# Two seven-product weight slabs: which engine forms the weight sums, where the raw blocks lie, and when the head squares run

## The chip, the cores and the metric

The kernel runs on one core of one Trainium2 chip. The metric is the device time of one execution in microseconds (us). A difference is read against the three runs of the kernel before, 1936.15 to 1937.51 us.

## The reference, cut to what matters

Two transformer blocks over 512 tokens of width 1024 in float32. The change touches the even layer of the second one:

```python
h = rmsnorm_2(x, pre_g)
u = h @ w_in.astype(jnp.float32)
qa, ka, va, oa, za, ia, fa, qb, kb, vb, zb = split_cols(u, EVEN_SPLITS)
...
ha = mlstm(qa.reshape(hs), ka.reshape(hs), va.reshape(hs), ig, lf)
ha = jax.nn.sigmoid(oa) * ha
ya = head_norm(ha, hn_g, A_HEADS) * jax.nn.silu(za)
```

`oa` and `za` are 512 x 1024 each: 512 tokens, contraction over 1024, 1024 columns. `head_norm` divides each of the 4 heads (256 wide) of a token by the root of the mean of its squares.

## The kernel before, in words

Every weight matrix is read in raw blocks of 128 rows by 512 columns of float32 (256 KB). A block becomes two operands: a high part, made by ScalarE's cast (L766, `w_hi_of`), and a low part, raw minus high, made by GpSimd for ordinary slabs (L713) and by VectorE for the seven-product slabs (L2063). TensorE takes three matmuls for each product of blocks: high by high, high by low, low by high. High and low parts have eight places each, taken in turn by block number; a cast waits until the block eight before has been used by TensorE (`wait_used`). Raw blocks of ordinary slabs lie in a ring of eight slots, `w_raw`; a slot is loaded again by SyncE (L605) when the low part of the block that had it is made.

`oa` and `za` are computed by two slabs of class `Seven`, `lstm_o` and then `lstm_z`. Tokens, contraction and columns are each halved, which gives 2 x 2 quarters of the weight matrix, q11, q12, q21, q22, of four raw blocks each, and four quarters of the result. Seven products of quarters replace the usual eight, in the Strassen-Winograd manner. The weight operands, in the order of the products, are B11 = q11, T1 = q11 + q12, T2 = T1 + q22, B21 = q21, T3 = q12 + q22, B22 = q22, T4 = T2 + q21; the signs are in the token operands, which VectorE and ScalarE make ahead of the slabs. One product is 4 blocks x 2 token tiles x 3 matmuls = 24 matmuls of 512 columns. An ordinary slab of eight blocks has 12 matmuls for each.

The raw blocks before: B11, T1, T2 and T4 share one buffer of four blocks, `kept`, used by both slabs. q11 is loaded into it (L615), for the second slab only after T4 of the first has given up its blocks. GpSimd then adds q12 and later q22 with accumulating DMAs (`weight_sums`, L744), each block when VectorE has made the low part of the sum that it held. T3 and B22 lie in the ring; VectorE adds T3 = q12 + q22 there (`add_t3`, L2048) between the low parts of B21. q21 lies in `b21` (L622), and VectorE adds it for T4 (`add_t4`, L2053) between the low parts of T3.

Products are summed in PSUM: banks `work` 0 and 1 and `proj` 0 to 3. Between products ScalarE seeds T2's banks with a copy of B11's product (`b_from_a`, L1280) and saves T1's product (`own_from_c`, L1288); VectorE seeds B22's banks from T2's product (`c_from_b`, L2074), for which T3 waits, and forms the second quarter of the result from T3's product (`own_from_b`, L2081), for which T4 waits. As each quarter of the result is complete ScalarE applies the gate (`gate`, L1307) and VectorE multiplies (`gated_quarter`, L2096 and L2101).

Each engine's order is written out by hand: on ScalarE by the calls of `prepared_to`, `gate` and the copies, on VectorE by `rests`, `c_from_b`, `own_from_b` and `gated_quarter`. SyncE issues plain loads in one queue in order of blocks, GpSimd its DMAs in another. Ahead of the two slabs TensorE works off the slab `sb_q` (eight blocks); behind them come `sb_k`, whose first block is followed by the transposes of the gated heads (L2498), and `sb_v`. The head squares of `head_norm` (L1342) are ScalarE's, 16 of 128 x 256, eight before and eight after the T3 casts of the second slab, all in the table set that also holds the square root.

## Time and profile before

| | us |
|---|---|
| median of 3 runs | 1937.35 |
| lowest, highest | 1936.15, 1937.51 |
| profiled execution, its own time | 1936.78 |
| its span | 1935.0 |
| TensorE busy | 1915.9 |
| VectorE busy | 790.0 |
| ScalarE busy | 811.0 |
| GpSimd busy | 951.1 |

The span runs from the first to the last instruction of the execution; its own time is 1.78 us longer. Times of the trace are counted from the span's start. The two seven-product slabs lie between 1239.00 and 1323.96 us.

### The profile page before, as it was taken

The numbers are of one execution on the slowest core, as the hardware profiler recorded it, in microseconds if no ns is written. First come the engines' busy times: TensorE is split into PE (matmuls) and PEld (weight loads), VectorE is DVE, ScalarE is ACT, GpSimd is POOL, SyncE is SP. The second block draws the span as 40 slices with busy tenths as digits, with TensorE's granted clock in tenths as the row PEclk, the third lists the DMA queues.
The fourth block names the chain that finished last, engine by engine and source line by source line (L and its number), as shares of the span: only waits on it lengthen the run. The fifth ranks groups of instructions, "written<-read, shape, count | busy, mean of one in ns | idle before, by whom it ended". The sixth has DMA issues, their size and how long they took to land.

```text
span 1935.0 us, 25859 instructions
## 1 busy us (share of the span) xinstructions
PE 1915.9 (99%) x9142; PEld 1607.0 (83%) x9142; DVE 790.0 (41%) x1264; ACT 811.0 (42%) x1585; POOL 951.1 (49%) x1237
## 2 busy tenths in 40 slices
PE   9999999999999999999999999999999999999998
PEld 7878888998888988888889888877888888888887
DVE  2430321340123223323247854766356646014652
ACT  5522443423324333333356543355456646333332
POOL 5733544534365555665545733115344455555572
PEclk9999999999999999999999999999999999999999
DMA  6342433323133323333342320554222242333331
GB/s 233 104 107 54 123 88 87 88 66 85 57 109 109 121 88 92 100 106 103 98 131 70 106 76 23 131 136 125 61 77 71 71 136 74 101 92 93 96 111 54
DMA packets 102849, 186.44 MB, mean 96 GB/s; under 512 B 11068, under 2 KB 16808, under 8 KB 102750
## 3 DMA queue, kind: packets, MB, share of 16 engines
q1 hardware_dynamic: 94676, 170.41, 30.1%
q10 hardware_dynamic: 5770, 10.49, 1.7%
q0 software_dynamic: 2304, 4.20, 1.3%
q8 instruction: 64, 1.05, 0.2%
q14 instruction: 35, 0.29, 0.0%
HBM read 179.03 MB, written 6.02 MB: 96 GB/s over the span
## 4 chain that ended last, share of the span: by engine, by line
PE 90%; DVE 5%; ACT 2%; DMA 2%; issue 1%; POOL 0%; SPq 0%; DVEq 0%; ACTq 0%; POOLq 0%
PE proj L2325 26%; PE proj L2327 26%; PE proj L2326 26%; DMA arena<-in_w_in_ab 2%; PE work L2325 1%; PE work L2326 1%; PE work L2327 1%; PE work L2896 1%; PE work L2877 1%; DVE w_lo L2063 1%; PE work L2701 1%; ACT w_hi L766 1%; PE work L2498 1%; PE work L2852 1%; PE work L2420 1%
## 5 line engine op out<-in xcount | busy, mean ns | idle before, releaser
L713 POOL TENSOR_TENSOR w_lo<-w_raw,w_hi 128x256 fp32r<-128x256 f32 x1200 | 931.9, 809 | 877.6 <-ACT w_hi L766 761.8
L2325 PE MATMUL proj<-act_hi,w_hi 128*128 128x512 f32 (+1 forms) x1312 | 495.8, 378 | 0.6 <-DVE arena L1775 0.3
L2327 PE MATMUL proj<-act_hi,w_lo 128*128 128x512 f32 (+1 forms) x1312 | 490.4, 374 | 0.0
L2326 PE MATMUL proj<-act_lo,w_hi 128*128 128x512 f32 (+1 forms) x1312 | 490.3, 374 | 0.0
L766 ACT CAST w_hi<-w_raw 128x512 fp32r<-128x512 f32 x520 | 304.1, 619 | 398.9 <-PE proj L2327 369.7
L2325 PEld LDWEIGHTS proj<-act_hi,w_hi 128*128 128x128 f32 x1312 | 247.1, 188 | 44.6 <-DVE arena L1775 0.7
L2327 PEld LDWEIGHTS proj<-act_hi,w_lo 128*128 128x128 f32 x1312 | 247.0, 188 | 44.3
L2326 PEld LDWEIGHTS proj<-act_lo,w_hi 128*128 128x128 f32 x1312 | 247.2, 188 | 43.7 <-issue 0.5
L2325 PE MATMUL proj<-w_hi,act_hi 128*128 128x512 f32 x640 | 257.5, 402 | 1.2 <-DVE arena L2187 1.0
L2327 PE MATMUL proj<-w_hi,act_lo 128*128 128x512 f32 x640 | 250.2, 391 | 0.0
L2326 PE MATMUL proj<-w_lo,act_hi 128*128 128x512 f32 x640 | 249.9, 391 | 0.0
L2325 PEld LDWEIGHTS proj<-w_hi,act_hi 128*128 128x128 f32 x640 | 128.0, 200 | 25.3 <-issue 2.1
L2325 PE MATMUL proj<-w_hi,aux_hi 128*128 128x512 f32 x368 | 146.1, 397 | 2.9 <-ACT arena L904 1.9
L2327 PEld LDWEIGHTS proj<-w_hi,act_lo 128*128 128x128 f32 x640 | 128.0, 200 | 23.1
L2326 PEld LDWEIGHTS proj<-w_lo,act_hi 128*128 128x128 f32 x640 | 128.2, 200 | 22.8 <-issue 1.0
L2327 PE MATMUL proj<-w_hi,aux_lo 128*128 128x512 f32 x368 | 143.4, 390 | 0.0
L2326 PE MATMUL proj<-w_lo,aux_hi 128*128 128x512 f32 x368 | 143.3, 389 | 0.0
L1118 ACT CAST w_hi<-w_raw 128x512 fp32r<-128x512 f32 x96 | 57.4, 622 | 126.2 <-PE proj L2327 125.9
L1823 DVE TENSOR_TENSOR arena<-arena 128x512 f32<-128x512 f32 x32 | 26.3, 821 | 144.3 <-ACT arena L1088 144.3
L2307 DVE TENSOR_TENSOR arena<-arena 128x512 f32<-128x512 f32 x40 | 35.6, 890 | 120.2 <-ACT arena L1466 119.3
L2325 PEld LDWEIGHTS proj<-w_hi,aux_hi 128*128 128x128 f32 x368 | 69.1, 188 | 18.5 <-POOL w_lo L713 3.5
L2326 PEld LDWEIGHTS proj<-w_lo,aux_hi 128*128 128x128 f32 x368 | 69.1, 188 | 14.8 <-issue 0.7
(396 smaller groups left out, 2241.9 us busy)
## 6 DMA issues: line engine op xcount, KB each, us to landing
w_raw<-in_w_in SPq DMA_DIRECT2D x154, 256.0 KB, 2.7
w_raw<-in_w_in_ab SPq DMA_DIRECT2D x130, 256.0 KB, 2.7
w_raw<-in_w_mlp SPq DMA_DIRECT2D x128, 256.0 KB, 2.8
w_raw<-in_w_in_c SPq DMA_DIRECT2D x64, 256.0 KB, 2.7
w_raw<-in_w_out_ab SPq DMA_DIRECT2D x32, 256.0 KB, 2.8
w_raw<-in_w_out_c SPq DMA_DIRECT2D x32, 256.0 KB, 2.8
w_raw<-in_w_o_gla SPq DMA_DIRECT2D x16, 256.0 KB, 2.7
w_raw<-in_w_out SPq DMA_DIRECT2D x16, 256.0 KB, 2.7
```

The source lines that it names most:

```text
L713: ins = pool.tensor_tensor(w_lo[:, slot, c], raw_of(b)[:, c], w_hi[:, slot, c].bitcast(F32), ALU.subtract)
L766: act.copy(w_hi[:, b % RING, :], raw_of(b)).then_inc(hi_ready, 1)
L1118: act.copy(w_hi[:, b % RING, :], raw_of(b)).then_inc(hi_ready, 1)
L1823: vec.tensor_tensor(relu_sq[:, c % 2, :], relu[:, c, :], relu[:, c, :], ALU.mult).then_inc(squared, 1)
L2063: vec.tensor_tensor(w_lo[:, b % RING, :], raw_of(b), w_hi[:, b % RING, :].bitcast(F32), ALU.subtract)\
L2307: step(vec.tensor_tensor(dst[:, POOL_PAD:], src[:, POOL_PAD:], src[:, POOL_PAD - back:PADDED - back], ALU.add))
L2325: pe.matmul(out_, a_hi, b_hi, start=first, stop=False)
L2326: pe.matmul(out_, a_hi, b_lo, start=False, stop=False)
L2327: return pe.matmul(out_, a_lo, b_hi, start=False, stop=last)
L2420: ins = pe.transpose(work[:, 2 * (m % 2) + b, (k % 4) * P:(k % 4 + 1) * P], normed_x[name][:, m, k * P:(k + 1) * P], ident[:])
L2498: ins = pe.transpose(work[:, k % 4, m * P:(m + 1) * P], src[:, m, c:c + P], ident[:])
L2701: ins = pe.matmul(work[:, 3, t], att_v[g][:, kb, h * HD:(h + 1) * HD], att_pt[g][:, at * P:(at + 1) * P], start=(g == 0 and n == 0), stop= ...
```

## The change

The sums T2 and T4, which stand in a chain, are now VectorE's: `add_t2` between the low parts of T1, `add_t4` between those of B21. The accumulating DMAs make T1 and T3, each one behind the plain load of its first summand. B11, B21 and T3 lie in the ring, T3 being summed in its slot. `kept` holds T1, T2 and T4 and has a place of its own for each slab; `held` holds q22 for T2 and B22. Each slab has 20 plain loads where it had 16, and 8 accumulating DMAs as before. A ring slot that held B21 is loaded again when `add_t4` has read it. The head squares are made in four groups of four, after the gates of the first slab; scratch for them lies in free parts of the arena.

```diff
-        super().__init__(name, q11 + q12 + q22 + q21 + q12 + q22 + q21, 4)
+        super().__init__(name, q11 + q11 + 4 * [None] + q21 + q12 + q22 + 4 * [None], 4)
+        self.added = {T1: q12, T3: q22}
...
-            s.kept, s.b21, s.own = view(0, 4, NCOL), view(10240, 4, NCOL), view(2048, 2, NCOL)
+        for s, kept_at in zip(sevens, (0, 14336)):
+            s.kept, s.held, s.own = view(kept_at, 4, NCOL), view(10240, 4, NCOL), view(2048, 2, NCOL)
+        head_squares_at = (12288, 13312, 0, 1024)
...
                 if ring_no[b] >= RING:
-                    wait_lo(sp, ring_order[ring_no[b] - RING])
+                    before_ = ring_order[ring_no[b] - RING]
+                    s, j = blocks[before_]
+                    if isinstance(s, Seven) and j // 4 == B21:
+                        sp.wait_ge(block_added, 8 * sevens.index(s) + 4 + j % 4 + 1)
+                    else:
+                        wait_lo(sp, before_)
...
             def load_seven(s):
                 at = sevens.index(s)
-                if s is sevens[0]:
+                def ring_loads(p):
+                    for k in range(4):
+                        load(s.first_of(p) + k, s.sources[4 * p + k])
+                ring_loads(B11)
+                if at == 0:
                     sp.wait_ge(proj_full, end("lstm_core"))
                 for k in range(4):
-                    if s is not sevens[0]:
-                        wait_lo(sp, sevens[at - 1].first_of(T4) + k)
-                    sp.dma_start(s.kept[:, k, :], s.sources[k]).then_inc(kept_loaded[k], 16)
-                for p in (T3, B22):
-                    for k in range(4):
-                        load(s.first_of(p) + k, s.sources[4 * p + k])
+                    sp.dma_start(s.kept[:, k, :], s.sources[4 * T1 + k]).then_inc(kept_loaded[k], 16)
+                if at:
+                    ring_loads(B21)
                 for k in range(4):
-                    if s is not sevens[0]:
-                        sp.wait_ge(block_added, 8 * at - 4 + k + 1)
-                    sp.dma_start(s.b21[:, k, :], s.sources[4 * B21 + k]).then_inc(b21_loaded[k], 16)
+                    if at:
+                        wait_lo(sp, sevens[at - 1].first_of(B22) + k)
+                    sp.dma_start(s.held[:, k, :], s.sources[4 * B22 + k]).then_inc(held_loaded[k], 16)
+                if at == 0:
+                    ring_loads(B21)
+                ring_loads(T3)
...
             def weight_sums(s):
-                for p in (T1, T2):
-                    for k in range(4):
-                        wait_lo(pool, s.first_of(p - 1) + k)
-                        pool.dma_start(s.kept[:, k, :], s.sources[4 * p + k], accum_op=ALU.add).then_inc(kept_summed[k], 16)
+                for k in range(4):
+                    pool.wait_ge(kept_loaded[k], 16 * (sevens.index(s) + 1))
+                    pool.dma_start(s.kept[:, k, :], s.added[T1][k], accum_op=ALU.add).then_inc(kept_summed[k], 16)
+                for k in range(4):
+                    b = s.first_of(T3) + k
+                    pool.wait_ge(raw_loaded[place[b][1]], t3_loads[b])
+                    pool.dma_start(raw_of(b), s.added[T3][k], accum_op=ALU.add).then_inc(ring_summed[k], 16)
...
+            def head_squares(quarter):
+                act.wait_ge(lstm_gated, 2 * quarter + 2)
+                for m in range(2):
+                    tokens, i = (0, 2, 0, 2)[quarter] + m, (0, 1, 1, 0)[quarter]
+                    for h in (2 * i, 2 * i + 1):
+                        at, r = head_squares_at[quarter] + (2 * m + h % 2) * LSTM_HD, LSTM_HEADS * tokens + h
+                        ins = act.activation(view(at, LSTM_HD), lstm_h[:, tokens, h * LSTM_HD:(h + 1) * LSTM_HD], ACT.Square,
+                                             accum_out=stat[:, r:r + 1])
+                return ins
...
             gate(o_, 2, ACT.Sigmoid, lstm_gated)
+            head_squares(0)
             prepared_to(z_, T1, 3)
             gate(o_, 3, ACT.Sigmoid, lstm_gated)
+            head_squares(1)
             prepared_to(z_, T2, 3)
             b_from_a(z_)
+            head_squares(2)
             prepared_to(z_, B21, 3)
             own_from_c(z_)
-            act.wait_ge(lstm_gated, 2 * MT)
+            prepared_to(z_, T3, 3)
+            ins = head_squares(3)
             act.preload_act_table_set("sqrt_and_others")
-            head_squares(0)
-            prepared_to(z_, T3, 3)
-            step(head_squares(8))
+            step(ins)
...
-            def add_t3(s, k):
-                own, other = s.first_of(T3) + k, s.first_of(B22) + k
-                vec.wait_ge(raw_loaded[place[own][1]], t3_loads[own])
-                wait_raw(vec, other)
-                vec.tensor_tensor(raw_of(own), raw_of(own), raw_of(other), ALU.add).then_inc(block_added, 1)
+            def add_t2(s, k):
+                wait_raw(vec, s.first_of(B22) + k)
+                wait_lo(vec, s.first_of(T1) + k)
+                vec.tensor_tensor(s.kept[:, k, :], s.kept[:, k, :], s.held[:, k, :], ALU.add).then_inc(block_added, 1)
             def add_t4(s, k):
-                wait_raw(vec, s.first_of(B21) + k)
                 wait_lo(vec, s.first_of(T2) + k)
-                vec.tensor_tensor(s.kept[:, k, :], s.kept[:, k, :], s.b21[:, k, :], ALU.add).then_inc(block_added, 1)
+                vec.tensor_tensor(s.kept[:, k, :], s.kept[:, k, :], raw_of(s.first_of(B21) + k), ALU.add).then_inc(block_added, 1)
...
-                        if j // 4 == B21:
-                            add_t3(own, j % 4)
                         vec.wait_ge(hi_ready, b + 1)
...
-                        if j // 4 == T3:
+                        if j // 4 == T1:
+                            add_t2(own, j % 4)
+                        elif j // 4 == B21:
                             add_t4(own, j % 4)
```

## Rows read from the trace of the kernel before

**Rows 1.** The page: the span, and busy time of each engine.
```profile
span 1935.0 us, 25859 instructions
...
PE 1915.9 (99%) x9142; PEld 1607.0 (83%) x9142; DVE 790.0 (41%) x1264; ACT 811.0 (42%) x1585; POOL 951.1 (49%) x1237
```

**Rows 2.** Waits of TensorE: who for whom, total us, times, longest us.
```profile
PE proj L2472 <- ACT proj L1280: 4.5, 1, 4.5
...
PE proj L2472 <- DVE proj L2074: 1.3, 2, 1.1
```

**Rows 3.** Timeline of TensorE: start, duration (us), instruction, [idle before <- releaser].
```profile
1239.00 0.39 PE L2472 MATMUL work<-w_hi,act_hi 128*128 128x512 f32 x1
...
1249.88 0.47 PE L2472 MATMUL proj<-w_hi,aux_hi 128*128 128x512 f32 x1
...
1261.23 0.47 PE L2472 MATMUL proj<-w_hi,aux_hi 128*128 128x512 f32 x1 [0.22 <-DVE proj L2074]
...
1288.34 0.39 PE L2474 MATMUL proj<-w_hi,aux_lo 128*128 128x512 f32 x1
1293.20 0.77 PE L2472 MATMUL proj<-w_hi,aux_hi 128*128 128x512 f32 x1 [4.47 <-ACT proj L1280]
...
1297.87 0.39 PE L2474 MATMUL proj<-w_hi,aux_lo 128*128 128x512 f32 x1
...
1307.52 0.47 PE L2472 MATMUL proj<-w_hi,aux_hi 128*128 128x512 f32 x1 [1.10 <-DVE proj L2074]
...
1323.96 0.39 PE L2325 MATMUL proj<-act_hi,w_hi 128*128 128x512 f32 x1
...
1327.08 1.50 PE L2498 MATMUL work<-ident,arena 128*128 128x128 f32 x12 [0.25 <-DVE arena L2101]
```

**Rows 4.** One stretch: busy PE, PEld, DVE, ACT, POOL; clock, DMA share, GB/s.
```profile
1293.00:1298.00 5.00, 4.80 (x12) 3.83 (x13) 4.70 (x9) 4.37 (x9) 0.00 (x0) 0.53 0.12 34
```

**Rows 5.** Timeline of ScalarE, 1291 to 1302.
```profile
1291.95 0.62 ACT L766 CAST w_hi<-arena 128x512 fp32r<-128x512 f32 x1 [1.38 <-DMA arena<-in_w_in_ab]
1292.47 1.06 ACT L1280 COPY proj<-work 128x512 f32<-128x512 f32 x2
...
1297.31 1.28 ACT L1335 ACT_TABLE_LOAD   x1
1298.61 0.42 ACT L1342 ACTIVATE arena<-arena 128x256 f32<-128x256 f32 x1
...
1301.82 0.61 ACT L766 CAST w_hi<-arena 128x512 fp32r<-128x512 f32 x1
```

**Rows 6.** Timeline of VectorE, 1232 to 1330.
```profile
1232.98 2.49 DVE L2063 TENSOR_TENSOR w_lo<-arena,w_hi 128x512 fp32r<-128x512 f32 x4
...
1306.68 1.29 DVE L2074 TENSOR_TENSOR proj<-proj,arena 128x512 f32<-128x512 f32 x2
...
1319.79 10.65 DVE L2101 SCALAR_TENSOR_TENSOR arena<-arena,rstd 128x256 f32<-128x256 f32 x12
```

**Rows 7.** Timelines of SyncE and of GpSimd: their DMA issues, 1217 to 1288.
```profile
1217.42 1.75 SPq L615 DMA_DIRECT2D arena<-in_w_in_ab  x4
...
1267.12 4.74 SPq L615 DMA_DIRECT2D arena<-in_w_in_ab  x4
...
1233.98 3.71 POOL L744 DMA_DIRECT2D arena<-in_w_in_ab  x4 [39.15 <-DVE w_lo L2063]
...
1287.30 0.86 POOL L744 DMA_DIRECT2D arena<-in_w_in_ab  x1 [1.17 <-DVE w_lo L2063]
```

**Rows 8.** Line L744, the 16 accumulating DMAs: issue to landing.
```profile
DMA to landing us min/median/max: 4.2/6.6/9.1
```

**Rows 9.** Line L622, the 8 plain loads of q21: issue to landing.
```profile
DMA to landing us min/median/max: 5.8/9.3/15.7
```

**Rows 10.** DMA queues, 1200 to 1345: packets, MB, share of 16 engines.
```profile
q1 hardware_dynamic: 7344, 13.37, 29.9%
...
q0 software_dynamic: 2304, 4.20, 17.8%
```

More of the change, by code:

```diff
@@ L243, in plan_raw @@
         p, k = j // 4, j % 4
-        if kind == "seven" and p not in (T3, B22):
-            place.append(("b21" if p == B21 else "kept", k))
-            loads.append({B11: ("kept", k, 16 * (group + 1)), T1: ("kept_sum", k, 16 * (2 * group + 1)),
-                          T2: ("kept_sum", k, 16 * (2 * group + 2)), B21: ("b21", k, 16 * (group + 1)),
-                          T4: ("added", 0, 8 * group + 4 + k + 1)}[p])
+        if kind == "seven" and p in (T1, T2, B22, T4):
+            place.append(("held" if p == B22 else "kept", k))
+            loads.append({T1: ("kept_sum", k, 16 * (group + 1)), T2: ("added", 0, 8 * group + k + 1),
+                          B22: ("held", k, 16 * (group + 1)), T4: ("added", 0, 8 * group + 4 + k + 1)}[p])
         else:
@@ L255, in plan_raw @@
                 t3_loads[len(loads)] = slots[slot]
-                loads.append(("added", 0, 8 * group + k + 1))
+                loads.append(("ring_sum", k, 16 * (group + 1)))
             else:
@@ L400, in two_blocks @@
         lstm_h, gate_tmp = view(4096, MT, D), view(16384, 4, SEQ)
-        for s in sevens:
-            s.kept, s.b21, s.own = view(0, 4, NCOL), view(10240, 4, NCOL), view(2048, 2, NCOL)
+        for s, kept_at in zip(sevens, (0, 14336)):
+            s.kept, s.held, s.own = view(kept_at, 4, NCOL), view(10240, 4, NCOL), view(2048, 2, NCOL)
+        head_squares_at = (12288, 13312, 0, 1024)
         s_hi, s_lo = [[t[:, at:at + 2, :].rearrange("p a (b t) -> p (a b) t", t=2 * P) for t in pair for at in (0, 2)]
@@ L430, in two_blocks @@
         kept_loaded = [sem(f"kept_loaded{k}") for k in range(4)]
-        kept_summed, b21_loaded = [sem(f"kept_summed{k}") for k in range(4)], [sem(f"b21_loaded{k}") for k in range(4)]
+        kept_summed, ring_summed = [sem(f"kept_summed{k}") for k in range(4)], [sem(f"ring_summed{k}") for k in range(4)]
+        held_loaded = [sem(f"held_loaded{k}") for k in range(4)]
         block_added = sem("block_added")
@@ L546, in raw_of @@
             where, at = place[b]
-            return w_raw[:, at, :] if where == "ring" else (blocks[b][0].b21 if where == "b21" else blocks[b][0].kept)[:, at, :]
+            return w_raw[:, at, :] if where == "ring" else (blocks[b][0].held if where == "held" else blocks[b][0].kept)[:, at, :]
         def wait_raw(eng, b):
@@ L552, in wait_raw @@
             eng.wait_ge(block_added if what == "added" else
-                        {"ring": raw_loaded, "kept": kept_loaded, "kept_sum": kept_summed, "b21": b21_loaded}[what][at], n)
+                        {"ring": raw_loaded, "kept_sum": kept_summed, "ring_sum": ring_summed, "held": held_loaded}[what][at], n)
         def wait_used(eng, block):
```

9 lines of the change are left out of this document (1 added, 8 removed).

## The prediction

> **What bounds the kernel.** I began with the page's busy shares: TensorE is busy in 1915.9 of 1935.0 us [rows 1], so anything that isn't a wait of TensorE is hidden, and this change neither adds nor removes a matmul. All that can be won is TensorE's own lost time. The table of who waits for whom names it [rows 2]: 4.5 us behind ScalarE's copy on L1280 and 1.3 us in two waits behind VectorE's L2074; 0.25 us behind L2101 stands in the timeline [rows 3]. All three belong to the two seven-product slabs or to the transposes right behind them. So I went through TensorE's matmuls in order of time there [rows 3].
>
> The pitch first: from 1239.00 (first product) to 1249.88 (third) lie 48 matmuls, 0.2267 us each. Two slabs are 2 x 7 products x 4 blocks x 2 banks x 3 = 336 matmuls, 76.17 us at that pitch. The stretch takes 1239.00 to 1323.96 = 84.96 us: 8.79 us are lost. Where:
> - T2 of the second slab: 1288.34 to 1293.20 is 4.86 us, 4.63 more than a pitch.
> - Behind it the engine works slowly: 1293.20 to 1297.87 are 11 pitches, 4.67 us where 2.49 would do, 2.18 us lost. The granted clock is 0.53 there, near its lower level, 1.2 GHz [rows 4]; what came before is the idle time just counted.
> - T3 of the second slab. 1297.87 is the 12th matmul of T2; 36 remain of T2 and B21, so T3 should have started 37 pitches later, at 1306.26. It starts at 1307.52: 1.26 us lost.
> - T3 of the first slab. T2 starts at 1249.88, two products are 48 matmuls, so T3 was due at 1260.76 and starts at 1261.23: 0.47 us.
> - The rest, 8.79 - 4.63 - 2.18 - 1.26 - 0.47 = 0.25 us, are stretched pitches right after these waits.
> Outside the stretch, the transposes at 1327.08 come behind a first block of 12 matmuls that started at 1323.96 and should be followed at 1326.68: 0.40 us.
>
> Why the 4.9 us: ScalarE executes in order. Its copy L1280, which seeds T2's banks, starts at 1292.47, directly behind a cast of a T2 operand that began at 1291.95 [rows 5]. That cast waited for an accumulating DMA, and this DMA is issued by GpSimd only when VectorE has made the low part of the same T1 block, because T2 is summed over T1 in place. An accumulating DMA lands 4.2 to 9.1 us after its issue, median 6.6 [rows 8]; the last one of the slab is issued at 1287.30 [rows 7], when TensorE is one us from needing T2. T1's own accumulation hangs in the same way on B11, and the whole chain starts only when the previous slab has let go of its one buffer: SyncE's first load for the second slab goes out at 1267.12 [rows 7]. Why T3's 1.26 us: VectorE's L2074 at 1306.68 [rows 6] is queued behind low parts of T3, whose casts ScalarE makes from 1301.82 on, behind eight squares that started at 1298.61 [rows 5] and a table load, all of it late from the same DMA.
>
> **The change, part by part.** I take TensorE's ideal starts as due times: first slab T1 1244.4, T2 1249.9, B21 1255.3, T3 1260.8, B22 1266.2, T4 1271.6; second slab B11 1277.1, T1 1282.5, T2 1288.0, B21 1293.4, T3 1298.8, B22 1304.3, T4 1309.7, end 1315.2 (1239.00 plus 5.44 each). A cast may be made when the block eight places before has been used: for block k of product p that is 10.9 us before its own due time. So a chain costs something only if it is more than about 9 us late against its slot.
>
> T2 and T4 sums on VectorE. Per slab 8 adds leave (T3, T4) and 8 come (T2, T4): VectorE's load is unchanged. An add has the shape of a low part, and four of those take 2.49 us, 0.60 each [rows 6]. The adds of T2 now stand after each low part of T1, those of T4 after B21. First slab: VectorE has B11's low parts at 1235.5 [rows 6]; T1's casts are allowed from 1239.00 - 3 x 2.72 = 1230.8 on (12 matmuls per block in the slab before), so low part and add, three times, end at 1239.1; then the four query products to about 1241.8, T1's fourth pair 1243.0, T2's low parts from 1243.6: due 1249.9. Between T2's last low part and L2074 there are now 4 x 2 + 3 = 11 operations and not 14, and none of them waits for a DMA issued late; T3's third low part comes about 1255.2 and L2074 ends near 1256.5: due 1260.8. The 0.47 us go. Second slab: T2's sums are made at 1276 to 1281, T2's low parts by 1283; L1280 can start when B11's product is full, 1281.8, and ends by 1283.6: due 1288.0. The 4.63 us go, and with the idle the 2.18 us of low clock.
>
> Accumulating DMAs, again 8 per slab, now T1 and T3 and only behind their own plain load. For T1 of the first slab: load issued at 1217.4 [rows 7], accumulation some 3 us later instead of at 1233.98. From below: landed at 1226. From above: the slowest plain load, 15.7 us [rows 9], four issues (3.71 us for four [rows 7]), slowest accumulation 9.1 us [rows 8] on top of the last load at 1219.2 give 1247.7 for T1's fourth block, whose matmuls are due at 1248.5, after a cast and a low part (1.3 us): 0.5 us late at the very worst. I take the middle, T1 landed by 1234, cost zero, because the slowest rows come from bursts. T3 of the first slab: its slots come free with B11's low parts (1233.6 to 1235.5), load to about 1239, accumulation to 1248: castable from 1251.2. Second slab: T1 goes into a buffer of its own (14336) without a wait for slots, but in SyncE's order behind four B11 loads, each waiting for a T4 add of the first slab (1248 to 1252.7). Loads to 1257, accumulated by 1266: castable from 1273. T3: slots free at 1271 to 1275.5, accumulated by 1288: castable from 1289.3. That is the tightest, with 1.3 us to its slot and 9 to its due time.
>
> Eight more plain loads. In a window of 145 us 51 plain 256 KB loads took 29.9% of the 16 engines and 16 accumulating ones 17.8% [rows 10]: 0.85 and 1.61 us of all engines each. Two slabs were 32 x 0.85 + 16 x 1.61 = 53.0 us and become 59.8. The old second slab issued its 16 loads in one burst from 1267.12 with the accumulations on top; now the first four go out before 1217, as soon as sb_q's slots are free, and the rest spread to about 1276: 60 us of full load in some 75. Cost zero, at worst a part of the slack above.
>
> Squares by quarter. Sixteen squares stay, 0.40 us each. Before they were two groups of eight in front of T3 and B22; now four groups of four (1.7 us) after gates, the first three (ending near 1274, 1279.5 and 1285.3) ahead of casts that are due 1281.2, 1286.6 and 1292.0. In the second slab only four squares, the root and two table loads remain ahead of B22: ScalarE's T3 casts to 1292.6, this to about 1297.2, then T3's fourth cast by 1297.7, due 1302.9, and B22's by 1299.3, due 1304.3. L2074 now stands before them: near 1294.7, due 1298.8. The 1.26 us go. Should a change between square and sigmoid cost a table load (1.28 us each [rows 5]), two would stand at each of the first three stops, 2.6 us against some 7: zero either way.
>
> The transposes. They need the second slab's gated quarters 0 to 2. VectorE's twelve products for quarters 1 to 3 took 10.65 us from 1319.79 [rows 6], 0.89 each, started behind T4's last low part, 1.3 us after T4's start. Now that part comes at 1307.7, 2 us before T4's start, the eighth product at about 1314.9, and the transposes are due at 1317.9. The 0.40 us go too.
>
> Sum: 8.79 + 0.40 = 9.2 us, from which I leave 0.1 for stretched pitches: 9.1. The profiled execution took 1936.78 us (span 1935.0, 1.78 around it), so it becomes 1927.7; it lay 0.57 below the median of the three runs, 1937.35, from which the forecast is 1928.2.
>
> A rule speaks against it. What the rows show is that the accumulating DMAs went out when VectorE was free or nearly so, and that the slowest landed after 9.1 us [rows 8]; the first slab's T1 ones now go out at 1221 to 1225, inside VectorE's gapless run of sums up to 1233.
> The Trainium skill (SBUF — State Buffer, the warning "The 'DVE blocks DMA' trap (SWDGE)") says that descriptors of a DMA issued from GpSimd can't be written while VectorE holds the port pair that the two share. No row of this case shows such an overlap over a longer run. By this rule T1's accumulations would be held until VectorE runs dry, and the time would come out as the next paragraph has it.
> The rival from it, worked out from rows: VectorE is dry at 1235.5 [rows 6], since its next low part needs the held block; four accumulations then land from 4.2 us later [rows 8], 1239.7 to 1245, T1's first low part at 1241, due 1244.4; the fourth by 1246.3, due 1248.5. T2's low parts then end at about 1249.5, due 1249.9. Nothing is lost, but the slack of the first slab is gone; with 9.1 us in place of 4.2 T1's blocks are 3 us late, which costs about 3 us of idle and 1 of low clock.
>
> **Rivals.**
> 1. Only the large wait goes. ScalarE or VectorE stays a little late and the waits at the two T3 and at the transposes stay, or a new one of that size comes. For it: each of the small waits hangs on the order of both engines and not on a DMA alone. Against: the slacks above are 3 us and more. Gain 4.63 + 2.18 = 6.8 and less, down to 4: 1930.5 to 1933.3; taken at 1931.
> 2. Held accumulations in the first slab (the paragraph above, slow end): 9.1 - 4 = 5, 1932. Against: slow landings stood in bursts.
> 3. The wait moves. T3's chain (B11 low part, SyncE's load, accumulation) in the second slab comes late as T2's did: it must be 9 us later than worked out, and then costs idle and low clock as before, about 7 us; 1935, no change.
> 4. Slower. SyncE's queue is one: the second slab's T1 load stands behind B11 loads that wait for VectorE's T4 adds. If these adds, and with them T1's accumulations, land after 1282.5 rather than 1266, ScalarE is blocked in order, T1 and T2 both stall, and with clock loss it costs 10 us or more beyond the gain: 1939. It decides only if the chain slips by 16 us.
> 5. That it doesn't do what it says: the block order in the code shows T2 free of GpSimd, so only a misread would bring 1937.
>
> **How the numbers follow.** Forecast as worked out 0.73, rival 1 0.12, rival 2 0.05, rival 3 (with 5) 0.06, rival 4 0.04. The likeliest case alone spans 1927 to 1929.5. The range takes rivals 1 and 2 in and, below, the scatter of the runs: 1926.8 to 1932.5. A measurement tells 0.2%, 3.9 us, from no change; faster by more are the first three cases, less a little of rival 1: 0.89; within 0.2%: 0.07; slower: 0.04.
>
> **What would show it.** In the changed profile: no wait of TensorE behind L1280's counterpart, the stretch of 336 matmuls 76 to 77 us long, granted clock 1.00 in all of it, accumulating DMAs of the first slab issued near 1221 and landed before 1240, none issued after 1285, L2074's counterpart ended 4 us before each T3, transposes without a wait. Wrong it would be if a wait of TensorE on a weight part or a seed of over 1 us stood anywhere in the stretch, or if the time saved there came back as waits behind it.

## The result, and the profile after

| | before | changed |
|---|---|---|
| median of 5 runs each, us | 1936.26 | 1925.61 |
| lowest, highest | 1934.84, 1937.51 | 1924.87, 1927.61 |
| profiled execution, its own time | 1936.78 | 1927.61 |
| its span | 1935.0 | 1925.9 |

The ratio is 0.9947, with an interval of 0.9932 to 0.9961. The forecast was 1928.2 in a range of 1926.8 to 1932.5: the direction is right, and the time lies 1.2 us under the range. Between the two profiled executions the spans differ by 9.1 us, which is the sum of the prediction.

The page of the changed kernel: the span and busy times, to be held against [rows 1].
```profile
span 1925.9 us, 25859 instructions
...
PE 1912.8 (99%) x9142; PEld 1605.7 (83%) x9142; DVE 792.5 (41%) x1264; ACT 813.3 (42%) x1585; POOL 950.7 (49%) x1237
```
TensorE's waits in the changed kernel. Neither wait of [rows 2] has a counterpart; what leads the list now lies in the first 19 us and behind copies at about 1500 to 1560 us, far from the change, and waits of the same size stood there before.
```profile
PE proj L2342 <- ACT arena L920: 1.9, 1, 1.9
PE proj L2547 <- POOL eps_col L713: 1.8, 1, 1.8
PE proj L2342 <- DVE arena L2204: 1.0, 1, 1.0
```
TensorE's timeline: B11, T2 and T3 of the first slab, T2 and T3 of the second, and the transposes. They answer [rows 3], and no row carries a bracket.
```profile
1239.03 0.39 PE L2489 MATMUL work<-w_hi,act_hi 128*128 128x512 f32 x1
...
1249.91 0.39 PE L2489 MATMUL proj<-w_hi,aux_hi 128*128 128x512 f32 x1
...
1260.79 0.39 PE L2489 MATMUL proj<-w_hi,aux_hi 128*128 128x512 f32 x1
...
1287.99 0.39 PE L2489 MATMUL proj<-w_hi,aux_hi 128*128 128x512 f32 x1
...
1298.87 0.39 PE L2489 MATMUL proj<-w_hi,aux_hi 128*128 128x512 f32 x1
...
1317.91 1.47 PE L2515 MATMUL work<-ident,arena 128*128 128x128 f32 x12
```
Two stretches: busy PE, PEld, DVE, ACT, POOL; clock, DMA share, GB/s. The first holds both slabs, the second answers [rows 4].
```profile
1239.00:1315.20 76.20, 76.20 (x338) 63.07 (x337) 61.40 (x96) 55.86 (x114) 15.92 (x19) 1.00 0.60 148
1293.00:1298.00 5.00, 5.00 (x24) 4.14 (x23) 2.13 (x4) 4.94 (x12) 0.00 (x0) 1.00 0.55 180
```
The 336 matmuls take 76.2 us, the pitch of 0.2267 us throughout; the clock is 1.00, where [rows 4] had 0.53. From the first product to the transposes it is 78.88 us, before it was 88.08: 9.20 less. The spans differ by 9.1.

ScalarE, as [rows 5]: T2's seed (L1296) starts 10.4 us earlier than L1280 did.
```profile
1282.07 1.25 ACT L1296 COPY proj<-work 128x512 f32<-128x512 f32 x2
```
VectorE, as [rows 6]: L2091 is the counterpart of L2074, L2118 of L2101.
```profile
1255.51 1.29 DVE L2091 TENSOR_TENSOR proj<-proj,arena 128x512 f32<-128x512 f32 x2
...
1293.59 1.29 DVE L2091 TENSOR_TENSOR proj<-proj,arena 128x512 f32<-128x512 f32 x2
...
1307.83 7.14 DVE L2118 SCALAR_TENSOR_TENSOR arena<-arena,rstd 128x256 f32<-128x256 f32 x8
```
GpSimd's accumulating DMAs, as [rows 7]: T1's of the first slab, and the last of the second slab's.
```profile
1220.50 1.92 POOL L756 DMA_DIRECT2D arena<-in_w_in_ab  x2 [25.65 <-DMA arena<-in_w_in_ab]
1223.01 1.75 POOL L756 DMA_DIRECT2D arena<-in_w_in_ab  x2 [0.59 <-DMA arena<-in_w_in_ab]
...
1281.31 0.86 POOL L760 DMA_DIRECT2D w_raw<-in_w_in_ab  x1 [5.18 <-DMA w_raw<-in_w_in_ab]
```
Issue to landing of T1's accumulations in both slabs (L756), to be held against [rows 8]:
```profile
DMA to landing us min/median/max: 6.5/8.9/10.8
```
The queues from 1190 to 1345, a window 10 us longer than that of [rows 10]:
```profile
q1 hardware_dynamic: 8581, 15.64, 33.9%
q0 software_dynamic: 2304, 4.20, 16.3%
```

### The profile page after: what moved, and what is told of

It is laid out like the page before. It is cut to its first block, busy times and chain, and to the rows that moved or that the text cites. A ratio compares the mean times of both kernels' runs of the same rounds, so it can differ in the third digit from the quotient of the medians.

```text
span 1925.9 us, 25859 instructions
## 1 busy us (share of the span) xinstructions
PE 1912.8 (99%) x9142; PEld 1605.7 (83%) x9142; DVE 792.5 (41%) x1264; ACT 813.3 (42%) x1585; POOL 950.7 (49%) x1237
## 4 chain that ended last, share of the span: by engine, by line
PE 96%; DVE 2%; ACT 1%; DMA 0%; issue 0%; SPq 0%; POOL 0%; DVEq 0%; ACTq 0%
PE proj L2342 27%; PE proj L2344 27%; PE proj L2343 27%; PE work L2342 1%; PE work L2343 1%; PE proj L2490 1%; PE proj L2489 1%; PE work L2344 1%; PE proj L2491 1%; PE work L2913 1%; PE work L2894 1%; PE work L2718 1%; PE work L2515 1%; PE work L2869 1%; PE proj L2861 1%; PE work L2437 1%
## 5 line engine op out<-in xcount | busy, mean ns | idle before, releaser
L782 ACT CAST w_hi<-w_raw 128x512 fp32r<-128x512 f32 x528 | 309.8, 619 | 431.7 <-PE proj L2344 395.3
L1134 ACT CAST w_hi<-w_raw 128x512 fp32r<-128x512 f32 x96 | 57.4, 622 | 126.2 <-PE proj L2344 125.9
```

The lines of the kernel that those rows point to most:

```text
L782: act.copy(w_hi[:, b % RING, :], raw_of(b)).then_inc(hi_ready, 1)
L1134: act.copy(w_hi[:, b % RING, :], raw_of(b)).then_inc(hi_ready, 1)
```

## The experiments

All times are medians in us; n is the number of runs. "Stage" is the time in the profile from the first product to the transposes behind the second slab: 88.08 before, 78.88 changed. Each stage is that of one profiled execution. It leaves out the scatter of the starts: the first product starts anywhere from 1237.93 to 1240.53 in these traces, so where two kernels are compared below, times are counted from their first product. It does not leave out all scatter. Where the chain of DMAs is late, their landings move it: the first slab's code is the same in the kernel before and in experiments 3, 5, 6 and 9, and lost 0.60, 0.61, 0.65, 1.17 and 0.85 us there. Differences under about 1 us between such kernels say little. Theory W says that the gain is TensorE's waits in the stage with the slow pitches behind them.

### 1. The changed kernel again
No edit; a second comparison, with another profile.

> The changed kernel unchanged, timed again. Theory W (the gain is the waits and the low clock of the two slabs and nothing else, 9.2 us less 0.1 of tail): ratio near 0.9953, 9.1 us below before, and the 1.5 us more that the first comparison of medians had is scatter of the runs. Rival X (something outside the two slabs got faster too, which the profiled execution did not show because it was the slowest of its five): 10.3 to 10.7 us below again, and the stretch behind the transposes (607.9 us before) shorter by over 1 us in the new profile.

Measured: 1926.37 (n 5, 1925.23 to 1927.95), before 1935.27 (n 15, 1934.55 to 1937.69), ratio 0.9954 [0.9940, 0.9967]: 8.9 us. The stage is 78.88 again, and behind it 607.93 us follow (607.99 in the first profile, 607.92 before). The gain lies in the stage alone; the first comparison's 10.65 and this one's 8.9 lie on both sides of 9.1.

### 2. Squares in two groups again
```diff
-            head_squares(0)
...
-            head_squares(1)
...
-            head_squares(2)
...
-            prepared_to(z_, T3, 3)
-            ins = head_squares(3)
             act.preload_act_table_set("sqrt_and_others")
-            step(ins)
+            head_squares(0)
+            head_squares(1)
+            prepared_to(z_, T3, 3)
+            head_squares(2)
+            step(head_squares(3))
```


> The changed kernel with the head squares put back in two groups of eight around the T3 casts of the second slab; all else as changed. Theory W, by the worked order: ScalarE makes T3's first three casts by about 1296, L2074's counterpart ends near 1297.5, due 1298.9; T3's fourth cast near 1301, due 1302.9. No wait of TensorE, same time as the changed kernel within 0.5 us: the squares by quarter earn nothing by themselves once the DMAs are on time. Rival S (the 1.26 us at T3 were the squares'): TensorE waits 1.3 us at T3 of the second slab again, 1.3 us slower.

Measured: 1926.54 (n 5, 1925.45 to 1927.96), ratio 0.9956 [0.9942, 0.9969]; stage 78.95, no wait of TensorE in it. With the operands on time, the order of the squares earns nothing.

### 3. The squares alone
The kernel before, with only the squares by quarter (its four scratch places free at that time):
```diff
             gate(o_, 2, ACT.Sigmoid, lstm_gated)
+            head_squares(0)
...
             gate(o_, 3, ACT.Sigmoid, lstm_gated)
+            head_squares(1)
...
             b_from_a(z_)
+            head_squares(2)
```


> The kernel before with the squares by quarter alone. Theory W: the 4.6 us wait at T2 of the second slab and the 2.2 us at low clock stay; the 1.26 us at T3 go, because only four squares stand before L2074; 1.3 to 1.6 us below before. Rival S2 (T3's wait came from the late DMA alone): nothing gained.

Measured: 1933.21 (n 11, 1932.48 to 1934.38), ratio 0.9990 [0.9981, 0.9999]; stage 85.62, 2.46 less than before. TensorE's rows that carry a bracket in this kernel's stage: T3 of the first slab, T1 and T2 of the second.
```profile
1260.63 0.47 PE L2476 MATMUL proj<-w_hi,aux_hi 128*128 128x512 f32 x1 [0.24 <-DVE proj L2078]
...
1287.34 0.50 PE L2476 MATMUL proj<-w_hi,aux_hi 128*128 128x512 f32 x1 [0.61 <-DVE w_lo L2067]
1292.44 0.77 PE L2476 MATMUL proj<-w_hi,aux_hi 128*128 128x512 f32 x1 [3.44 <-ACT proj L1281]
```
The wait at T3 of the second slab is gone, that at T2 not: 1.03 us of it went, but 0.61 us of wait now stands at T1, and T2 starts only 0.12 us earlier. The 2.46 us are 1.2 at T3, 0.7 of slow pitches behind T2, 0.4 at the transposes and this 0.1. So the squares are worth about 2.5 us while T2 is late, and nothing once it isn't. The expectation, 1.3 to 1.6 us, had only the part at T3.

### 4. One buffer for both slabs
The changed kernel, with one buffer (at 14336) for both slabs: T1's blocks of the second slab are loaded when the first slab has done with it.
```diff
-        for s, kept_at in zip(sevens, (0, 14336)):
+        for s, kept_at in zip(sevens, (14336, 14336)):
...
+                    if at:
+                        wait_lo(sp, sevens[at - 1].first_of(T4) + k)
                     sp.dma_start(s.kept[:, k, :], s.sources[4 * T1 + k]) ...
```


> The changed kernel with one buffer for T1, T2, T4 of both slabs again, so that the second slab's T1 load waits for T4's low parts of the first (about 1269 on). Sums T2 stay on VectorE. Theory W: T1 is accumulated at 1276 to 1284 instead of 1266, T2's sums about 8 us later; the copy L1280's counterpart is behind T2's third cast near 1285 and ends by 1286.5, due 1288.0: wait of at most 0.5 us, time within 1 us of the changed kernel. Rival B (the buffer of its own is what took the wait away): 4 us and more of wait at T1 or T2 of the second slab, with low clock behind it, 5 us and more slower than the changed kernel.

Measured: 1926.78 (n 5, 1925.34 to 1928.38), ratio 0.9959 [0.9945, 0.9972]; stage 78.88, no wait. T1's four accumulations of the second slab go out at 1265.58 to 1274.15, 27.6 to 36.2 us after the first product (1237.99), and not 17.2 to 20.0 us after it as in the changed kernel; T2's seed starts 45.65 us after it (1283.64) instead of 43.04 (1282.07). At 1.1 us long the seed must start by 47.9 for T2 at 48.96: a slack of 2.2 us is left of 4.8, and the buffer of its own earns nothing by itself.

### 5. TensorE kept busy through the wait
The kernel before, with 16 matmuls into a bank nobody reads, where TensorE waits for T2 of the second slab. It asks whether the low clock's 2.18 us can be had apart from the wait.
```diff
                                 elif p == T2:
+                                    if at and m == 0:
+                                        for _ in range(16):
+                                            pe.matmul(work[:, 2, :], act_hi[:, 0, 0:P], act_hi[:, 1, :], start=True, stop=True)
                                     pe.wait_ge(b_seeded, 2 * at + m + 1)
```


> The kernel before with 16 matmuls of 512 columns, whose result nobody reads, put into TensorE's wait at T2 of the second slab (3.6 us of the 4.6 us wait). Theory C (the 2.18 us behind the wait are the price of the idle time by way of the clock): the wait stays until the same moment, the granted clock stays at 1.00 behind it, the 11 slow pitches go: about 2 us below before. Rival N (the slow pitches come from something else, such as operands that arrive late): slow pitches as before, no gain.

Measured: 1935.33 (n 11, 1933.44 to 1937.24), before 1935.18, ratio 0.9998 [0.9989, 1.0007]; stage 88.72. The bracketed rows of the second slab, and two stretches of it (columns as above):
```profile
1291.71 0.50 PE L2475 MATMUL proj<-w_hi,aux_hi 128*128 128x512 f32 x1 [0.16 <-ACT proj L1280]
...
1306.08 0.47 PE L2475 MATMUL proj<-w_hi,aux_hi 128*128 128x512 f32 x1 [2.65 <-DVE proj L2074]
```
```profile
1291.70:1296.70 5.00, 4.99 (x22) 4.13 (x23) 4.74 (x9) 4.42 (x8) 0.00 (x0) 1.00 0.12 37
1306.00:1311.00 5.00, 4.92 (x15) 3.91 (x16) 3.56 (x7) 4.97 (x9) 0.00 (x0) 0.66 0.38 105
```
Behind T2 the clock is full now, and TensorE could start T3 65.1 us after the first product where it was 67.3. L2074 comes only 0.6 us earlier (1305.25, 67.1 us after the first product, for 1306.68, 67.7 after), so the wait there grows from 1.10 to 2.65 us and the slow pitches stand behind it instead. The expectation had the clock right and its worth, 2 us, wrong. In the kernel before, the low clock cost little of its own: VectorE's and ScalarE's lateness stood behind it.

### 6. The same filler with the squares by quarter
Experiments 3 and 5 together, 14 matmuls: here nothing should be late at T3.

> The kernel before with squares by quarter (as in a3_squares_only) and 14 unread matmuls in TensorE's wait at T2 of the second slab. In b1_filler the filler removed the slow pitches behind T2, but TensorE then waited 2.8 us at T3, which hung on ScalarE's squares. Theory M (the two losses overlapped: the slow pitches cost nothing while T3 waits anyway): with T3 free, the filler now pays, 1.4 to 1.8 us below a3_squares_only. Rival N2 (clock loss is never worth its pitches here): no difference to a3_squares_only.

Measured: 1933.33 (n 11), before 1935.99 (n 27), ratio 0.9986 [0.9977, 0.9995]; stage 86.53, against 85.62 for the squares alone.
```profile
1293.00:1298.00 5.00, 4.96 (x22) 4.12 (x23) 3.78 (x7) 5.00 (x15) 0.00 (x0) 1.00 0.06 10
```
```profile
1305.53 0.47 PE L2479 MATMUL proj<-w_hi,aux_hi 128*128 128x512 f32 x1 [1.31 <-DVE proj L2078]
```
The clock is full behind T2, and the time again goes into a wait at T3, which experiment 3 had not. VectorE is the next bound: from the low part of T2's last block, at 1295.65, it works without a gap up to L2078, which ends at 1305.97. The two traces differ ahead of the filler too: T2 starts 0.8 us later than in experiment 3, 0.6 of it from the first slab. From T2's start on they lose the same, 1.7 and 1.6 us. The gain of 1.4 to 1.8 us that was expected isn't in this trace; the intervals of the two ratios are too wide to exclude it.

### 7. The accumulations with the queues quiet
The changed kernel; SyncE holds the twelve loads behind T1's (for B22, B21 and T3) until T1's accumulations have landed. VectorE runs gapless through both cases.
```diff
                 if at:
                     ring_loads(B21)
+                else:
+                    for k in range(4):
+                        sp.wait_ge(kept_summed[k], 16)
```


> The changed kernel; in the first slab SyncE issues the loads of q22, B21 and T3 only when T1's four accumulations have landed. These accumulations went out at 1220.5 to 1224, inside VectorE's gapless sums, beside twelve plain loads, and took 8.0 to 10.8 us. Theory Q (the queue of other transfers made them slow): 4 to 5.5 us each now, VectorE as busy as before. Rival V (VectorE holds the port and GpSimd can't write descriptors, the rule of the Trainium skill weighed in the prediction): still 8 us and more, landed near or after 1233. The loads behind come some 9 us later, within their slack: TensorE's stretch stays at 76.2 us.

Measured: 1925.59 (one run); stage 78.88, no wait. Issue to landing of T1's four accumulations in this kernel, the first two and then the last three:
```profile
DMA to landing us min/median/max: 4.3/4.9/5.6
...
DMA to landing us min/median/max: 5.4/5.6/6.1
```
and of the first two, and then of all four, in the changed kernel:
```profile
DMA to landing us min/median/max: 8.0/8.6/9.2
...
DMA to landing us min/median/max: 8.0/9.3/10.8
```
VectorE in the quiet kernel, over the time of these accumulations (issued 1219.54 to 1223.5), has no gap:
```profile
1219.14 1.23 DVE L2058 TENSOR_TENSOR arena<-act_hi,act_lo 128x1024 f32<-128x1024 f32 x1
1220.40 1.23 DVE L2133 TENSOR_TENSOR early<-early,arena 128x1024 f32<-128x1024 f32 x1
1221.55 1.22 DVE L2058 TENSOR_TENSOR arena<-act_hi,act_lo 128x1024 f32<-128x1024 f32 x1
```
Landing nearly twice as fast with the same VectorE: what stretched it were the loads beside it. Theory Q holds; the reading rests on one trace.

### 8. T2's sums by DMA again
The changed kernel, with T2 made over T1 by accumulating DMA instead of by VectorE's add; T1 stays ahead of use.
```diff
+                for k in range(4):
+                    wait_lo(pool, s.first_of(T1) + k)
+                    pool.dma_start(s.kept[:, k, :], s.sources[4 * B22 + k], accum_op=ALU.add).then_inc(kept_summed[k], 16)
...
-                        if j // 4 == T1:
-                            add_t2(own, j % 4)
-                        elif j // 4 == B21:
+                        if j // 4 == B21:
```


> The changed kernel with T2's sums made by accumulating DMAs over T1 again, each after T1's low part, T1 itself still loaded and accumulated ahead. Theory E (the wait came from two links in a row, T1 after B11's low part and T2 after T1's): with the first link gone T2's accumulations of the second slab go out at 1276 to 1282 and land 5 to 7 us later, third cast near 1286.5, the seeding copy at 1287, T2 due 1288.0: 0 to 0.8 us of wait, within 1 us of the changed kernel. Rival L (T2's own link is what costs): 3 us and more of wait at T2 and low clock behind it, 5 us slower than the changed kernel.

Measured: 1925.49 (n 5, 1925.34 to 1926.78), ratio 0.9950 [0.9936, 0.9964]; stage 78.88, no wait. T2's accumulations go out up to 1280.08, 42.2 us after the first product (1237.93) and not 48.3 as in the kernel before, and the seed 45.6 after it, with 2.2 us of slack. VectorE's sums earn nothing by themselves either.

### 9. The loads of the second slab in another order
The kernel before, with T3's and B22's loads of the second slab ahead of B11's, so that fewer transfers run beside the accumulations.
```diff
+                if at:
+                    ring_loads()
                 for k in range(4):
                     if s is not sevens[0]:
                         wait_lo(sp, sevens[at - 1].first_of(T4) + k)
                     sp.dma_start(s.kept[:, k, :], s.sources[k]).then_inc(kept_loaded[k], 16)
+                if at == 0:
+                    ring_loads()
```


> The kernel before; for the second slab SyncE issues the eight ring loads (T3, B22) ahead of q11's loads, when their slots are free (about 1257 to 1266), so that no burst of twelve loads from 1267 runs beside T1's and T2's accumulations. Nothing else. Theory D (contention: each of the two links took 6.6 to 9.1 us instead of 4 to 5.5): both links 2 to 3 us shorter, wait at T2 0 to 1.5 us instead of 4.6, little low clock; 4 to 6 us below before in the two places, less what T3's wait keeps (it hangs on the squares only partly). Rival K (the chain of two links after B11's low part is too long whatever the queue): wait at T2 stays over 3 us, gain under 2 us.

Measured: 1933.28 (n 11, 1931.99 to 1938.10), ratio 0.9987 [0.9978, 0.9996]; stage 87.89.
```profile
1292.14 0.47 PE L2479 MATMUL proj<-w_hi,aux_hi 128*128 128x512 f32 x1 [1.64 <-ACT proj L1287]
...
1306.39 0.77 PE L2479 MATMUL proj<-w_hi,aux_hi 128*128 128x512 f32 x1 [2.66 <-DVE proj L2081]
```
The wait at T2 falls from 4.47 to 1.64 us, and T2's four accumulations land in 4.3 to 5.3 us where they took 6.6 to 7.0: much of the wait was contention. The stage shrinks by only 0.2 in this trace, since the wait at T3 and the slow pitches behind it take the rest. But the profiled execution is the slowest of the eleven, 1938.10, and not like the others. An execution's own time is the stage, the rest of the span, and 1.7 us around it. Estimated from the changed kernel's fastest run, 1924.87 less 78.88 and 1.7, the rest takes 1844.3 us at least; with it a stage of 87.89 would give 1933.9 and more. Seven of the eleven runs are faster. By this estimate their stages were shorter, and the medians differ by 2.7 us (0.8 to 4.3 by the interval). By the medians contention alone is worth about that, less than the 4 to 6 us of Theory D and more than Rival K gave it.

### 10. All the links together
Experiments 4 and 8 together, and T1's accumulations behind B11's low parts, as before. The squares, the accumulations for T3 and the sources of B11, B22 and T4 stay as changed.
```diff
                 for k in range(4):
+                    wait_lo(pool, s.first_of(B11) + k)
                     pool.wait_ge(kept_loaded[k], 16 * (sevens.index(s) + 1))
                     pool.dma_start(s.kept[:, k, :], s.added[T1][k], accum_op=ALU.add).then_inc(kept_summed[k], 16)
```


> The changed kernel with the whole old chain put back: T1's accumulations wait for B11's low parts, T2's are DMAs after T1's low parts, and T1's buffer is shared by both slabs. What stays of the change: B11 and B21 in the ring, so that the loads are spread in time, T3 by DMA, squares by quarter. Theory D (contention and the late start of B11's own load made the wait): T2's third cast of the second slab near 1285.5, copy ended by 1287, wait 0 to 1 us; within 1.5 us of the changed kernel. Rival K (the links made the wait): 3 to 5 us of wait at T2, low clock behind it, 5 us and more slower than the changed kernel.

Measured: 1934.56 (n 11, 1931.79 to 1937.77), ratio 0.9993 [0.9984, 1.0002]; stage 86.48, 7.60 more than changed. TensorE's bracketed rows, and the stretch behind the last of them:
```profile
1246.33 0.47 PE L2493 MATMUL proj<-w_hi,aux_hi 128*128 128x512 f32 x1 [1.54 <-DVE arena L2129]
...
1252.31 0.47 PE L2493 MATMUL proj<-w_hi,aux_hi 128*128 128x512 f32 x1 [0.27 <-ACT proj L1302]
...
1294.05 0.47 PE L2493 MATMUL proj<-w_hi,aux_hi 128*128 128x512 f32 x1 [3.38 <-ACT proj L1302]
```
```profile
1294.00:1299.00 5.00, 4.95 (x15) 3.96 (x16) 3.79 (x8) 5.00 (x16) 1.72 (x2) 0.66 1.10 188
```
GpSimd and ScalarE in this kernel show the chain of [rows 5, 7] whole again: an accumulation, the low part, the next accumulation, the cast behind it, the seed behind the cast.
```profile
1278.22 0.86 POOL L759 DMA_DIRECT2D arena<-in_w_in_ab  x1 [2.52 <-DVE w_lo L2084]
...
1285.98 0.86 POOL L762 DMA_DIRECT2D arena<-in_w_in_ab  x1 [1.08 <-DVE w_lo L2084]
```
```profile
1292.80 0.62 ACT L788 CAST w_hi<-arena 128x512 fp32r<-128x512 f32 x1 [1.40 <-DMA arena<-in_w_in_ab]
1293.33 1.06 ACT L1302 COPY proj<-work 128x512 f32<-128x512 f32 x2
```

TensorE's first bracketed row above, at T1 of the first slab, has no counterpart in the kernel before. T1's accumulations of the first slab go out at 1234.18 as they did then (1233.98), but with more loads in flight (182 GB/s from 1234 to 1238, where it was 79 before) they land later. Issue to landing of these four, here and before:
```profile
DMA to landing us min/median/max: 6.7/8.4/9.5
...
DMA to landing us min/median/max: 4.2/6.1/7.2
```
So 2.32 of the 7.60 us are lost in the first slab, where the kernel before lost 0.60, and 5.28 in the second, where it lost 8.20 (the split stands behind experiment 12). Rival K's 3 to 5 us at T2 came about; Theory D's 0 to 1 did not.

### 11. Of the links, T1 taken ahead
Experiment 10 without its last edit: T1's accumulations wait for their own loads only; one buffer, T2 by DMA.

> As c5_all_links (shared buffer, T2 by DMA after T1's low part), but T1's accumulations again wait only for their own plain load. c5 lost 7.6 us against the changed kernel in its trace (1.7 at T1 of the first slab, 3.5 and low clock at T2 of the second). Theory J (the wait needs both links in a row; breaking either one is enough): no wait at T1 of the first slab, T2 of the second 0 to 1 us, within 1.5 us of the changed kernel. Rival K2 (T2's link with a late shared buffer is enough for the wait): 3 us and more at T2, 5 us slower than the changed kernel.

Measured: 1929.41 (n 5, 1926.92 to 1929.89), before 1935.94, ratio 0.9965 [0.9952, 0.9979]; stage 82.58. What is left is 1.83 us idle before T2 of the second slab, and slow pitches behind it. Both sides missed: Theory J had at most 1 us of wait and 1.5 us in all, Rival K2 3 us of wait and 5 in all. T2's link with the late shared buffer costs 3.70.
```profile
1289.09 0.47 PE L2492 MATMUL proj<-w_hi,aux_hi 128*128 128x512 f32 x1 [1.83 <-ACT proj L1301]
```
```profile
1289.00:1294.00 5.00, 4.91 (x15) 3.90 (x16) 3.79 (x7) 5.00 (x16) 0.28 (x1) 0.66 0.93 166
```

### 12. Of the links, T2 taken to VectorE
Experiment 10 with T2's sums on VectorE; one buffer, T1's accumulations behind B11's low parts.

> As c5_all_links, but T2's sums on VectorE as in the change; T1's accumulations wait for B11's low parts and the buffer is shared. This is what moving the T2 sums to VectorE is worth by itself. Theory J: T2 of the second slab waits 0 to 1.5 us instead of 3.5; the 1.7 us at T1 of the first slab stay, since VectorE's query products stand behind T1's low parts; 2 to 3.5 us slower than the changed kernel, 4 us and more faster than c5. Rival T (T1's link alone is enough for the wait): 3 us and more at T1 or T2 of the second slab, as slow as c5.

Measured: 1931.53 (n 11, 1931.06 to 1933.94), ratio 0.9980 [0.9971, 0.9989]; stage 84.11. T2 is on time, and the waits stand at T1, mostly in the first slab:
```profile
1246.22 0.49 PE L2492 MATMUL proj<-w_hi,aux_hi 128*128 128x512 f32 x1 [2.63 <-DVE arena L2128]
...
1290.64 0.50 PE L2492 MATMUL proj<-w_hi,aux_hi 128*128 128x512 f32 x1 [0.40 <-DVE w_lo L2081]
```

Theory J had T2 right and the price wrong: 5.23 us, not 2 to 3.5. Nearly all of it stands in the first slab, as in experiment 10. The second slab's first matmul shows the split; at the pitch it comes 38.08 us after the first product. Before (first product 1239.00), experiment 10 (1239.19) and this one (1237.99):
```profile
1277.68 0.39 PE L2472 MATMUL work<-w_hi,act_hi 128*128 128x512 f32 x1
...
1279.59 0.39 PE L2493 MATMUL work<-w_hi,act_hi 128*128 128x512 f32 x1
...
1280.56 0.39 PE L2492 MATMUL work<-w_hi,act_hi 128*128 128x512 f32 x1
```

| lost against the pitch, us | first slab | second slab | transposes |
|---|---|---|---|
| before | 0.60 | 8.20 | 0.40 |
| 10, both links | 2.32 | 5.28 | 0 |
| 11, T2's link only | 0 | 3.70 | 0 |
| 12, T1's link only | 4.49 | 0.74 | 0 |
| changed | 0 | 0 | 0 |

In the second slab, where the kernel before lost its time, T2's link is the costly one: 3.70 us alone, and T1's adds 1.58 to it and costs 0.74 alone, all three with the shared buffer. T1's link costs most in the first slab, by a wait that the kernel before did not have. No version here beats the changed kernel, and within the two slabs nothing is left to win but fewer matmuls: 336 at their pitch fill them.

## Why the prediction was right in its mechanism and wrong in its level

**The sum.** Summed 9.1 us; the profiled pair shows 9.1 in the span (1935.0 to 1925.9) and 9.17 in its own time (1936.78 to 1927.61, where the prediction had 1927.7). Each place came out as worked out, within 0.4 us: T2 of the second slab without its 4.63, the clock at 1.00 in place of 0.53, T3 of the second slab on the pitch, T3 of the first at 1260.79 (due 1260.76), the transposes without a wait. The seed started at 1282.07 and ended by 1283.3 (forecast 1281.8 to 1283.6), L2091 ended at 1256.8 and 1294.9 (forecast 1256.5 and 1294.7), the accumulations went out from 1220.50 and up to 1281.31.

**The step that failed** is the last one: "it lay 0.57 below the median of the three runs, 1937.35, from which the forecast is 1928.2", and with it the lower end, "below, the scatter of the runs: 1926.8". Three runs within 1.4 us were taken for the level and for its scatter. The five runs of the comparison itself have a median of 1936.26, the four later sets of 15 to 27 runs medians of 1935.18 to 1935.99. Of all 77 runs, 1933.79 to 1938.36 with a median of 1935.81, eight are as slow as 1937.35. So the base was 1.1 to 2.2 us too high. The rest of the miss is scatter of the changed kernel: 1936.26 less 9.1 is 1927.2, and the five runs gave 1925.61; the repeated comparison gives 1926.37, and three other kernels with the same stage or one 0.07 longer have medians of 1925.49 to 1926.78 (experiments 2, 4, 8). The range left no room below for either.

The scatter has places. Outside the stage the span takes 1844.7 to 1848.5 us in the 14 profiles of this case; before, changed, its repeat and experiment 10 lie at 1846.9 to 1847.3, nine others at 1844.7 to 1845.9, experiment 9 at 1848.5. Two places make it. The first product starts anywhere from 1237.9 to 1240.5, by waits of TensorE at 8 to 19 us behind ScalarE (0 to 2.1) and GpSimd (0.9 to 1.8). And behind the transposes lie 606.8 or 607.9 us: profiles with the longer one have a wait of 1.0 to 1.1 us behind VectorE's copies (L2204, in the second fence above), the others don't. What decides over that wait in an execution wasn't found. A profiled pair cancels this only when both fall on the same side, as here by luck.

**The terms are not separate prices.** The prediction added 4.63, 2.18, 1.26 and 0.47, and the sum holds because all causes were removed at once. As prices of single edits they would have been wrong. The low clock's 2.18 us taken alone gained nothing (experiment 5), since L2074 was late by as much; 2.8 us off the T2 wait gained 0.2 in the trace of experiment 9 and about 2.7 in its medians; the squares took 2.5, more than the 1.26 put down to them, by the slow pitches and the transposes besides the T3 wait (experiment 3), and became worth nothing behind the other edits (experiment 2).

**What each part of the change is worth.** T2's lateness came from two accumulations in a row behind VectorE's low parts, from a late start, and from the loads beside them (experiment 9). Take back the buffer or T2's sum alone and slack of 2.2 us remains (experiments 4, 8). Take back both and T1's link, and the stage is 7.6 us longer (experiment 10), but this is not the old loss coming back whole: 5.28 of the 8.20 us return in the second slab, and 2.32 us stand in the first slab, where before it was 0.60. The 2.9 us that do not return in the second slab are not taken apart; the squares, T3's sums and the order of the loads stayed as changed in that kernel. T1's link alone with a buffer of its own was not run.

**Rivals.** Rival 1 would leave a wait in the stage, and there is none. Rival 2 and the rule put behind it: the accumulations issued at 1220.50 landed 8.0 to 10.8 us later while VectorE was gapless up to 1233, which looks like the rule until the loads are held back; then they land in 4.3 to 6.1 us with VectorE just as full. The Trainium skill (SBUF — State Buffer, "The 'DVE blocks DMA' trap (SWDGE)") gives that lockout for the time in which VectorE runs an operation of its two-port fast modes, such as a float32 `tensor_copy` within SBUF. VectorE's instructions here are float32 sums and differences of two tensors, so the prediction applied the rule more widely than that passage states it. With these operations the trace shows no such wait; no run here has a fast-mode copy beside an accumulation. Rivals 3 and 4: T3's accumulations of the second slab were issued by 1281.31 and landed at most 6.6 us later, and T1's, issued by 1259.0, at most 9.9 later, 1268.9, where 1266 was worked out. They are many microseconds short of the points from which either rival decides. One bound of mine was too low: 9.1 us for the slowest accumulation, where 10.8 was seen; no slack was used up by it. The shares were 29.9% and 17.8% of 145 us [rows 10] and are 33.9% and 16.3% of 155 us: 52.5 us of all engines for 15.64 MB of plain loads, where 43.4 us went to 13.37 MB, so a plain load costs 0.88 us and not 0.85.

## To carry to other kernels

Where each operand is made by a DMA that waits for an engine's work on the one before, it is the landings in a row that make the wait, and loads beside them stretch each landing: take one link and the late start away and slack appears, and further edits against the same chain earn nothing. Putting a link back doesn't give its old price either; here it made a new wait in the first slab. A profile of one execution can be the odd one out, so hold its stage against all the runs (experiment 9). Summing the waits of the bounding engine gives the gain of a change that removes all their causes, not the price of one edit; for one, ask what is late right behind. The level needs its own care: a gain of 9.1 us worked out exactly still missed the range, because three runs stood for the base and its scatter.

## What was not expected of the hardware

- An accumulating DMA of 256 KB landed in 4.3 to 6.1 us with no further load issued until it had landed and in 8.0 to 10.8 with twelve plain loads issued beside it, VectorE equally busy in both.
- TensorE's granted clock fell towards its lower level, 1.2 GHz, behind waits that were short, and not by their length alone: after 1.83 us idle the stretch of 5 us behind it shows 15 matmuls and a granted clock of 0.66 (experiment 11), after 1.64 us 22 matmuls and 1.00 (experiment 9). After 2.66 us it was 12 and 0.50 (experiment 9), after 2.65 us 15 and 0.66 (experiment 5).
- Unread matmuls in place of the wait kept the clock at 1.00 and brought no time, because VectorE was as late (experiments 5, 6).
